# Placing the movable SBUF buffers of a transformer block at 64 instead of 128 modulo 256 bytes

## Time and profile before

| | |
|---|---|
| three runs | 1719.5, 1721.49, 1721.71 us |
| profiled execution, its own time | 1720.11 us |
| its span, first to last instruction | 1718.4 us |
| mean granted TensorE clock | 0.998 |
| TensorE busy / weight loads | 1692.7 / 1363.7 us |
| VectorE / ScalarE / GpSimd busy | 1008.8 / 740.4 / 164.3 us |
| moved by DMA | 419.35 MB, mean 244 GB/s |

### The profile page before, as it was taken

How to read it: one execution, slowest core, us unless ns; L and a number is a source line. 1 busy time by engine, 2 the same in 40 slices (tenths; PEclk the granted TensorE clock), 3 DMA queues, 4 the chain that set the end, 5 groups by cost and what they waited for, 6 DMA issues and landing times.

```text
span 1718.4 us, 21875 instructions
## 1 busy us (share of the span) xinstructions
PE 1692.7 (99%) x8109; PEld 1363.7 (79%) x8109; DVE 1008.8 (59%) x1146; ACT 740.4 (43%) x832; POOL 164.3 (10%) x179
## 2 busy tenths in 40 slices
PE   6999999999999999999999999999999999999998
PEld 2458888887878888888888788888888888888886
DVE  2446767748966777666665764454545454444444
ACT  3324222217555454445446654444444444443442
POOL 0011000000046355220000000000000000000000
PEclk9999999999999999999999999999999999999999
DMA  9999999978988666656776566666666666766662
GB/s 366 377 381 372 353 343 363 347 279 304 374 302 275 197 220 197 212 148 222 227 263 218 183 224 192 186 193 185 191 187 189 189 188 189 262 193 193 195 193 90
DMA packets 183676, 419.35 MB, mean 244 GB/s; under 512 B 12960, under 2 KB 13328, under 8 KB 173760
## 3 DMA queue, kind: packets, MB, share of 16 engines
q1 hardware_dynamic: 167680, 375.45, 66.4%
q0 software_dynamic: 7184, 27.71, 4.9%
q10 hardware_dynamic: 8752, 15.38, 2.4%
HBM read 397.99 MB, written 20.50 MB: 244 GB/s over the span
## 4 chain that ended last, share of the span: by engine, by line
PE 96%; DVE 2%; DMA 1%; issue 1%; ACT 0%; POOL 0%; SPq 0%; DVEq 0%; POOLq 0%; ACTq 0%
PE ps L1639 28%; PE ps L1643 28%; PE ps L1651 28%; PE ps L1721 2%; PE ps L1695 2%; DMA raw<-in_w_mod 1%; PE ps L1737 1%; PE ps L1941 1%; PE ps L1925 1%; PE ps L1979 1%; PE ps L1866 0%; PE ps L1684 0%; DVE xr_t L424 0%; PE ps L2057 0%; PE ps L2044 0%
## 5 line engine op out<-in xcount | busy, mean ns | idle before, releaser
L1055 DVE TENSOR_TENSOR w_lo<-raw,w_hi 128x1024 fp32r<-128x1024 f32 x486 | 602.6, 1243 | 501.2 <-ACT w_hi L648 500.9
L648 ACT ACTIVATE w_hi<-raw 128x1024 fp32r<-128x1024 f32 x488 | 515.7, 1060 | 774.0 <-PE ps L1651 758.7
L1639 PE MATMUL ps<-w_hi,h_hi 128*128 128x512 f32 x1440 | 452.6, 395 | 0.0
L1643 PE MATMUL ps<-w_hi,h_lo 128*128 128x512 f32 x1440 | 445.3, 389 | 0.0
L1651 PE MATMUL ps<-w_lo,h_hi 128*128 128x512 f32 x1440 | 392.4, 389 | 0.0
L1643 PEld LDWEIGHTS ps<-w_hi,h_lo 128*128 128x128 f32 x1440 | 270.3, 188 | 56.8
L1651 PEld LDWEIGHTS ps<-w_lo,h_hi 128*128 128x128 f32 x1440 | 270.2, 188 | 56.4
L1639 PEld LDWEIGHTS ps<-w_hi,h_hi 128*128 128x128 f32 x1440 | 266.8, 188 | 55.6 <-ACT w_hi L648 1.5
L1067 DVE SCALAR_TENSOR_TENSOR acc<-wm,csil,acc 128x2048 f32<-128x2048 f32 x60 | 141.0, 2350 | 60.9 <-DMA wm<-in_w_mod 60.8
L1639 PE MATMUL ps<-w_hi,hid_hi 128*128 128x512 f32 x352 | 109.8, 389 | 0.0
L1643 PE MATMUL ps<-w_hi,hid_lo 128*128 128x512 f32 x352 | 109.7, 389 | 0.0
(11 more groups left out here) (315 smaller groups left out, 1390.5 us busy)
## 6 DMA issues: line engine op xcount, KB each, us to landing
raw<-in_w_in SPq DMA_DIRECT2D x184, 512.0 KB, 6.5
wm<-in_w_mod SPq DMA_DIRECT2D x64, 1024.0 KB, 7.1
raw<-in_ffn_w_gate SPq DMA_DIRECT2D x88, 512.0 KB, 4.4
raw<-in_ffn_w_up SPq DMA_DIRECT2D x88, 512.0 KB, 4.4
raw<-in_ffn_w_down SPq DMA_DIRECT2D x88, 512.0 KB, 4.6
raw<-in_w_mod SPq DMA_DIRECT2D x64, 512.0 KB, 8.1
raw<-in_w_out SPq DMA_DIRECT2D x32, 512.0 KB, 4.8
px<-stage ACTq DMA_DIRECT2D x44, 256.0 KB, 6.1
```

The source lines that it names most:

```text
L648: act.activation(w_hi[:, j % SPLIT, :, :], raw[:, j % RAW, :, :], ACT.Copy).then_inc(w_high, 1)
L1055: dve.tensor_tensor(w_lo[:, j % SPLIT, :, :], raw[:, j % RAW, :, :], w_hi[:, j % SPLIT, :, :].bitcast(F32), ALU.subtract).then_inc(w_low, 1)
L1639: pe.matmul(o, hi[:, kk, c], w_h[:, e, :], start=kk == 0, stop=False)
L1643: pe.matmul(o, lo[:, kk, c], w_h[:, e, :], start=False, stop=False)
```

## The change

One line. `base` is the first address from the cursor on that is 64 modulo 256, where it was the first that is 128 modulo 256. With the cursor at 133568 it goes from 133760 to 133696, and every buffer made by `reg` lies 64 bytes lower. No instruction, no semaphore, no size and no order is changed.

```diff
--- before.py
+++ after.py
@@ -137,7 +137,7 @@
         stats = keep("stats", [P, 2, MT, 6])
         mv = keep("mv", [P, 2, MT, 2])
         hr = keep("hr", [P, 2, MT, 1])
-        base = (cursor[0] + 127) // 256 * 256 + 128
+        base = (cursor[0] + 191) // 256 * 256 + 64
         K = 1024
 
         def reg(name, shape, kb, dt=F32):
```

## The result

The changed kernel took 1729.45 us (median of 6 runs, 1728.87 to 1731.28) against 1721.16 us before in the same session (6 runs, 1719.5 to 1721.91). The ratio is 1.0052, with a 95% interval of 1.0041 to 1.0062: 8.3 us slower, and outside the range that was given.

A forecast was written before the change was run, and what follows sets the result against it. TensorE was taken to bound the kernel, and every term was taken as zero: 1720.11 us for the profiled execution plus 0, stated as 1721.5 us since that execution lay 1.4 us under the median, range 1717.5 to 1727.

The forecast's parts named there:

- What bounds the kernel: Whole kernel: TensorE, busy 1692.7 of 1718.4 us and 96% of the chain, so only its work or waits count.
- Point 1: 2112 weight loads from moved buffers: 188 ns each, hidden beside 226.7 ns matmuls; taken as 0, upper end 146 us.
- the clash of TensorE's two reads: Weight-load reads hold up moving-operand reads; a shift doubles the loss on 2112 matmuls: 28 us slower, 1749.6 us; chance 0.04.
- the 13.3 ns of every matmul: Large products: 226.7 ns per 512-column matmul, against 213.3 at one column per cycle; the price of both clash rivals.
- The argument against it: Lines 1790 and 1791: 7.0 ns lost over 256 columns, one part in 16 as for 512, as a fixed tax would be.
- Point 2: Moving operands in moved buffers, head products and w_ahead0 to w_ahead4: at most 6.9 us together, taken as zero.
- Point 3: VectorE and ScalarE on moved tiles: start does not matter within 3%; exposed stretches at most 2.7 us, taken as zero.
- Point 4: DMA into moved buffers, 64 chunks of 1 MB: covered, TensorE doesn't wait; 2.9 us if the cover were gone.
- comparison of rope with r_q: 256 KB loads: rope at 0 modulo 256 took 4.6 us, r_q at 128 took 4.4; the aligned one is not faster.
- rival of 128-byte pieces: Head stage and two exposed stretches: reads in pieces of 128 bytes cost 9.6 us, 1731.1 us; chance 0.06.
- The reverse clash, faster: TensorE's reads: the same clash goes away with the shift, 28 us faster, 1693.3 us; chance 0.03.
- the change does nothing: Placement of base: with the cursor elsewhere it could move by +192 instead of -64; time the same; chance 0.01.

The follow-up runs named there:

- e1: Against the kernel before, only base moved, to 0 modulo 256 instead of 128; 1736.55 us, ratio 1.0094.
- e2: Against the kernel before, only base moved, to 192 modulo 256 instead of 128; 1736.39 us, ratio 1.0091.
- e3: Against the kernel before, w_hi and w_lo alone moved to 64 modulo 256, with h and base still at 128; 1761.7 us, ratio 1.0238.
- e4: Against the kernel before, everything (raw, w_hi, w_lo, h, stage, base) moved to 64 modulo 256; 1721.22 us, ratio 1.0003.
- e6: Kernel before, but the down product loads 64 of 128 stationary columns and leaves out the rest of that output; 1724.2 us, ratio 1.0021.
- e11: Kernel before, but the down product loads 32 of 128 stationary columns and leaves out the rest of that output; 1726.55 us, ratio 1.0032.
- e10: Against the kernel before, o placed 240 and hid 256 bytes from the moving operand's start, counted modulo 256 and 512; 1721.62 us, ratio 1.0002.
- e5: Against the kernel before, h_hi, h_lo and base moved to 64 modulo 256, raw and w kept at 128; 1733.95 us, ratio 1.0081.

## Why the prediction was wrong, step by step

**What bounds the kernel** was right, and it is what made the rest matter: with TensorE on the chain for 96%, 2.2 ns on each of some 1500 matmuls and 4.5 ns on some 960 are 7.7 of the 8.3 us.

**Point 1 failed.** It asked whether the weight load would get longer, found 39 ns of room, and took nothing. The load did not get longer: 188 ns before and after. But a load that is hidden beside a matmul can slow the matmul: its turn went from 226.7 to 228.9 ns, and to 231.2 where h and hc take turns. The cost lies in the instruction that does the hiding, and the room counts for nothing. The rows called nearest, the transposes of ctx_w and gw_cols, were near in address only. They are fp32 products of 128 columns, not fp32r of 512, and they still take the same time at lags that cost the fp32r pair 2 to 7 ns: the transposes of hid_n follow each other at 109.0 ns before (lag 0), in the change (192) and in e1 (128), and at 108.8 in e2 (64).

**The rival that held was the clash of TensorE's two reads**, with a chance of 0.04. That a shift of one operand against the other slows the matmul stands, and so does the sign; e3 and e4 show it. That the 13.3 ns of every matmul are this clash does not follow: with half the load they grew to 16.7. The price was mis-sized: 13.3 ns for each of 2112 matmuls, where 2.2 ns was measured at o and hid and 4.5 ns in the context blocks, 8.3 us instead of 28. The argument against it misled me. That the loss was one part in 16 for two shapes was read as a fixed tax; e6 and e11 show a larger one for the same moving operand. The very rows of that argument, lines 1790 and 1791, moved with the change, from 113.7 to 116.7 ns. And the sentence that no row shows fp32r operands with unlike phases should have set the chance. Where the trace holds no case of the thing in dispute, a chance of 0.04 is not supported by it.

**Point 2** (moving operands in moved buffers) came out at zero for the head products that it priced, but they don't test the rival: both operands of each lie in moved buffers, so their lag is 0 before and after, and in every run here. The case that point 2 had right in front of it is `w_ahead0` to `w_ahead4`, moving operands 64 bytes lower against an h that stayed, a lag of 64. In the fifth of them four matmuls in a row take 0.94 us (1000.13 to 1001.07 us) where they took 0.92 (993.67 to 994.59). TensorE also waits among them, and the whole stretch went only from 18.25 to 18.31 us, so zero was near enough. **Point 3** was right: medians of 287 and 286 ns for the reads of cum, and what lay exposed in the opening gave 0.1 us. The 0.9 us of the latent blocks no point had priced. Most of it lies in large products that read h at an unchanged lag, in the turns after a break. That their fit with the load is disturbed there is my reading; it was not tried by itself.

**Point 4** was right: TensorE gained no wait, and the 1 MB chunks landed in 7.1 us as before. Its comparison of rope with r_q proves little either way: it is one load against four, and both are written into SBUF.

**The rival of 128-byte pieces fell** with e4 and e1, which lies on a multiple of 128 and is slower. The reverse clash, faster, fell too: no lag gave less than 226.7 ns. That the change does nothing fell with the result.

The Trainium skill, "SBUF — State Buffer", section "Who interferes with whom", gives TensorE two read ports, one for the moving operand and one for weight loads, independent of each other, and says that TensorE never waits on anyone. The runs speak against that for this pair: moving w_hi and w_lo by 64 bytes against everything else makes a matmul take 233.3 instead of 226.7 ns, with the engines beside it doing the same work. The measurement decides. The two ports may well exist; what the runs exclude is that the two streams don't affect each other.

**Still open:** what the two reads meet in, why the lag of 192 is milder, why stationary buffers at lags 0 and 192 in turn cost more than 192 alone, and why one and the same lag can run at two paces (240 in e10, 0 at line 1790).

## What to carry to other kernels

Where fp32r matmuls with a fresh 128 x 128 load each set the time, give the stationary and the moving buffers the same start modulo 256 bytes; the absolute place doesn't matter (64 and 128 modulo 256 were tried). Here that is worth up to 41 us of 1721 and costs at most 255 bytes. And when an operation is "hidden", price also what it does to the operation that hides it.

## What was not expected of the hardware

- The turn of a matmul of 512 fp32r columns depends on where its stationary operand's buffer starts against the moving one's: 226.7 to 234.3 ns by the lag, the same again 256 bytes on in the places tried.
- A slot that alternates between stationary buffers at lags 0 and 192 costs 231.2 ns per matmul, more than 228.9 with both at 192. With 0 and 64 it is 231.7, less than the 233.3 of 64 alone.
- The pace can outlast its cause: 64-column loads beside 256 fp32r columns at lag 0 ran at 113.3 ns a turn in e5 and at 116.7 in the change, where they follow others at lag 192.
- With 64 or 32 stationary columns instead of 128 the matmul's turn was longer, 230.0 and 231.7 instead of 226.7 ns, although the load itself, in the records, fell from 188 to some 134 and 108 ns.
- fp32 transposes (109.0 ns a turn at lags 0, 128 and 192) showed none of this, nor did VectorE's and ScalarE's reads of cum. For the other fp32 head products it is not known, since their two operands always moved together.
